# A two-block transformer kernel on one core: modulation weights spread between the layer mixers' products, the last norm and loads in one block, up weights laid out by chunk

## What is computed

```python
for l in range(2):                                   # first block
    mod = silu(c) @ ada_w[l] + ada_b[l]              # 6 x 1024 columns: "modulation"
    h = rms_norm(x) * (1 + mod.scale1) + mod.shift1
    p = h @ w_in                                     # latents, q/k, v, gate, branch gates
    y_mla, y_mlstm = latent attention(p), mLSTM(p)   # 8 heads each
    m = sigmoid(p.br0) * (y_mla @ w_br0) + sigmoid(p.br1) * (y_mlstm @ w_br1)
    x = x + mod.gate1 * (m @ w_out)
    h = rms_norm(x) * (1 + mod.scale2) + mod.shift2
    a, b = split(conv(h @ ffn_w_up))                 # 2 x 2816 columns
    x = x + mod.gate2 * ((gelu(a) * b) @ ffn_w_down)
x = rms_norm(x) * final                              # end of the first block
x = second_block(x, ctx, ...)                        # two recurrences, attention, experts
```

## Time and profile before

| | us |
|---|---|
| median of 3 runs | 2472.73 |
| profiled execution | 2476.21 |
| its span | 2474.4 |
| PE busy | 2041.8 (83%) |
| DVE busy | 1448.3 (59%) |
| ACT busy | 1109.7 (45%) |
| one `ada` piece, issue to landing (median) | 5.2 |
| `final`, issue to landing | 3.5 |
| the second block's `consts`, issue to landing | 4.7 |

### The profile page before, as it was taken

How to read it: one execution, slowest core, us unless ns; L and a number is a source line. 1 busy time by engine, 2 the same in 40 slices (tenths; PEclk the granted TensorE clock), 3 DMA queues, 4 the chain that set the end, 5 groups by cost and what they waited for, 6 DMA issues and landing times. The chain is left out here.

```text
span 2474.4 us, 37498 instructions
## 1 busy us (share of the span) xinstructions
PE 2041.8 (83%) x15206; PEld 1719.4 (69%) x15206; DVE 1448.3 (59%) x1787; ACT 1109.7 (45%) x1308; POOL 144.2 (6%) x134
## 2 busy tenths in 40 slices
PE   4788888698878888789748986798629999999997
PEld 4676666697767666589637774686527878788785
DVE  0274424585446342478425857854438878788786
ACT  0262423464254332356326434212317767677674
POOL 0000000000000000000000632630000000000000
PEclk8798789798989788889878998798759999999998
DMA  8742354453364245264423220000238989899896
GB/s 328 280 149 86 130 194 180 148 193 110 114 228 135 80 162 221 77 232 143 162 86 121 69 74 9 13 18 10 72 137 322 374 291 372 300 348 377 288 371 230
DMA packets 196926, 447.59 MB, mean 181 GB/s; under 512 B 10657, under 2 KB 58401, under 8 KB 196769
## 3 DMA queue, kind: packets, MB, share of 16 engines
q1 hardware_dynamic: 196768, 445.42, 50.7%
HBM read 444.33 MB, written 1.05 MB: 180 GB/s over the span
## 5 line engine op out<-in xcount | busy, mean ns | idle before, releaser
L212 DVE TENSOR_TENSOR me_wlow<-me_w,me_whigh 128x2048 fp32r<-128x2048 f32 x195 | 442.6, 2289 | 101.6 <-ACT me_whigh L207 101.2
L207 ACT ACTIVATE me_whigh<-me_w 128x2048 fp32r<-128x2048 f32 x195 | 372.1, 1918 | 124.3 <-PE ps L220 124.0
L212 DVE TENSOR_TENSOR mix_wlow<-mix_w,mix_whigh 128x1024 fp32r<-128x1024 f32 (+2 forms) x116 | 140.0, 1212 | 154.7 <-ACT mix_whigh L207 154.5
L218 PE MATMUL ps<-me_whigh,me_xhigh 128*128 128x512 f32 x512 | 207.0, 404 | 13.3 <-PEq L119 13.3
L218 PE MATMUL ps<-up_xhigh,up_whigh 128*128 128x256 f32 x704 | 202.9, 288 | 16.8 <-DVE up_wlow L212 16.8
L220 PE MATMUL ps<-me_whigh,me_xlow 128*128 128x512 f32 x512 | 202.2, 395 | 0.0
L219 PE MATMUL ps<-me_wlow,me_xhigh 128*128 128x512 f32 x512 | 202.1, 395 | 0.0
L219 PE MATMUL ps<-up_xlow,up_whigh 128*128 128x256 f32 x704 | 201.6, 286 | 0.0
L220 PE MATMUL ps<-up_xhigh,up_wlow 128*128 128x256 f32 x704 | 201.5, 286 | 0.0
L207 ACT ACTIVATE mix_whigh<-mix_w 128x1024 fp32r<-128x1024 f32 (+2 forms) x116 | 121.2, 1047 | 133.4 <-DMA mix_w<-w_mix 109.0
L218 PEld LDWEIGHTS ps<-up_xhigh,up_whigh 128*128 128x128 f32 x704 | 137.4, 195 | 18.6 <-issue 16.2
(11 more groups left out here) (664 smaller groups left out, 4426.3 us busy)
## 6 DMA issues: line engine op xcount, KB each, us to landing
me_w<-w_exp_gate SPq DMA_DIRECT2D x34, 2048.0 KB, 9.5
me_w<-w_exp_up SPq DMA_DIRECT2D x34, 2048.0 KB, 10.1
me_w<-w_exp_down SPq DMA_DIRECT2D x32, 2048.0 KB, 10.1
mix_w<-w_mix SPq DMA_DIRECT2D x108, 512.0 KB, 4.3
mix_w<-ada_w SPq DMA_DIRECT2D x96, 512.0 KB, 5.2
up_w<-ffn_w_up SPq DMA_DIRECT2D x40, 1024.0 KB, 7.1
ada_w<-ada_first SPq DMA_DIRECT2D x12, 2048.0 KB, 22.3
sec_w<-w_in SPq DMA_DIRECT2D x31, 512.0 KB, 3.7
```

The lines of the kernel that those rows point to most:

```text
L207: return nc.scalar.activation(high, x, ACT.Copy)
L212: return nc.vector.tensor_tensor(low, x, high.bitcast(F32), ALU.subtract)
L218: nc.tensor.matmul(out, lh, rh, start=start, stop=False)
```

## The change

- `Pieces` gets a second ring, `mix_aside`, of three slots for the pieces that are not split; `mix_w` shrinks from five slots to four. SP still issues all fetches from one queue, now in an order sorted by planned times (`fetch_order`).
- The `ada` pieces are spread: four stand at the start, then mostly one after each weight piece (pattern 1, 1, 1, 1, 0, 1, 1, 2, 0). The sum of a chunk is planned later, at +4.4 instead of +3.0 behind the last piece of the chunk, and the bias at +5.2 instead of +4.0.
- Products rotate over three banks, and modulation chunks have bank 3 alone. The last eight products (`out`) use all four.
- `yT[1]` shares the space of `latT`.
- The up weights are laid out on the host so that one chunk is one DMA with a contiguous run in each partition.
- The final norm, its load and the loads of the second block stand in one block, `first_output`.

```diff
+        if wholes:
+            self.aside = core.sb(mem, f"{what}_aside", [P, wholes, KD * P])
...
+    def fetch_order(self):
+        planned, order = self.split_at(), []
+        for split, slots in ((True, self.raws), (False, self.wholes)):
+            users = [p for p, row in enumerate(self.rows) if row[4] == split]
+            for i, p in enumerate(users):
+                before = users[i - slots] if i >= slots else None
+                if before is None:
+                    when = 1.5 * i + 1.0 * split
+                else:
+                    when = planned[before] + 2.0 if split else self.at[before] + 0.8
+                order.append((when, p, before))
+        return sorted(order)
...
-        pieces = Pieces(core, sem, mem, "mix", SLICE, 5, 4, 8.0)
+        pieces = Pieces(core, sem, mem, "mix", SLICE, 4, 4, 8.0, 3)
...
-                pieces.add("ada", spare[0], ada[spare.pop(0)], 0.9, False)
-        for _ in range(12):
-            modulation_piece()
+                pieces.add("ada", spare[0], ada[spare.pop(0)], cost, False)
...
+        pieces.clock = 3.5
+        for _ in range(4):
+            modulation_piece(0.9)
         pieces.clock = max(pieces.clock, 11.0)
...
+            weights(name, i, cost)
+            for _ in range((1, 1, 1, 1, 0, 1, 1, 2, 0)[n % 9]):
+                modulation_piece()
...
-        units = Units(core, sem, "mix", 4, names)
+        units = Units(core, sem, "mix", 3, names)
+        out_units = Units(core, sem, "out", 4, out_names[3 - rest:3] + out_names[:3 - rest] + out_names[3:])
+        ada_units = Units(core, sem, "ada", 1, [f"ada{j}" for j in range(ADA_PIECES // 4)], 3)
...
-                            for s in range(2):
-                                c0 = s * D_FF + j * pairs * P
-                                sp.dma_start(raw[:, j % STAGES, a:b, s * pairs * P:(s + 1) * pairs * P],
-                                             w[:, a:b, c0:c0 + pairs * P])\
-                                    .then_inc(first[n] if j == 0 else landed[j % STAGES], 16)
+                            sp.dma_start(raw[:, j % STAGES, a:b, :], w[j, :, a:b, :])\
+                                .then_inc(first[n] if j == 0 else landed[j % STAGES], 16)
...
+def first_output(core, I, x, coming):
+        with nc.Block(no_gpsimd_drain=True) as block:
+            @block.sync
+            def _(sp):
+                sp.dma_start(final[:, :], I["final"].to_broadcast([P, DM])).then_inc(final_here, 16)
+                for dst, src in coming:
+                    sp.dma_start(dst, src).then_inc(here, 16)
+                sp.wait_ge(here, 16 * len(coming))
```

More of the change, by code:

```diff
@@ L734, in halves, with slot, has_landed @@
         return [self.view(b, slot, p) for b in self.split]
-    def whole(self, p):
-        return self.view(self.raw, p % self.raws, p)
+    def slot(self, p):
+        split = self.rows[p][4]
+        if not split:
+            ring, landed, n, i = self.aside, self.aside_landed, self.wholes, p - self.splits[p]
+        else:
+            ring, landed, n, i = self.raw, self.landed, self.raws, self.splits[p] - 1
+        return ring, landed[i % n], i % n, i // n
+    def whole(self, p):
+        ring, _, slot, _ = self.slot(p)
+        return self.view(ring, slot, p)
+    def has_landed(self, eng, p):
+        _, landed, _, turn = self.slot(p)
+        eng.wait_ge(landed, 16 * (turn + 1))
     def arrived(self, pe, p):
@@ L742, in arrived @@
         else:
-            pe.wait_ge(self.landed[p % self.raws], 16 * (p // self.raws + 1))
-    def fetch(self, sp, between=None):
[L746 to L750, removed]
+            self.has_landed(pe, p)
+    def fetch_order(self):
[6 more added lines that the diff above has]
+                    when = 1.5 * i + 1.0 * split
+                else:
+                    when = planned[before] + 2.0 if split else self.at[before] + 0.8
+                order.append((when, p, before))
+        return sorted(order)
+    def fetch(self, sp, between=None):
+        for n, (_, p, before) in enumerate(self.fetch_order()):
+            if between and n in between:
+                between[n]()
+            split = self.rows[p][4]
+            if before is not None and split:
                 sp.wait_ge(self.low, self.splits[before])
-            elif before >= 0:
+            elif before is not None:
                 sp.wait_ge(self.done, before + 1)
-            sp.dma_start(self.whole(p), src).then_inc(self.landed[p % self.raws], 16)
+            sp.dma_start(self.whole(p), self.rows[p][2]).then_inc(self.slot(p)[1], 16)
     def split_at(self):
@@ L760, in split_at @@
             if row[4]:
-                when, before = self.at[p] - self.lead, p - self.raws
-                if before >= 0:
-                    when = max(when, out[before] + 1.7 if self.rows[before][4] else self.at[before] + 2.5)
+                when = self.at[p] - self.lead
+                if len(users) >= self.raws:
+                    when = max(when, out[users[-self.raws]] + 1.7)
                 if len(users) >= self.parts:
@@ L1043, in opened @@
             if name == "ada":
-                return [f"ada{i // 4}"] if i % 4 == 0 else []
+                return []
             if name == "br":
@@ L1049, in opened @@
             if name == "out":
-                return [f"out{i // 4}{t}" for t in both] if i % 4 == 0 else []
+                return []
             return [f"{name}{t}" for t in both] if i == 0 else []
         names = [unit for name, i, *_ in pieces.rows for unit in opened(name, i)]
-        units = Units(core, sem, "mix", 4, names)
+        units = Units(core, sem, "mix", 3, names)
+        out_names = [f"out{c}{t}" for c in range(2) for t in range(TT)]
+        before_out = names[-3:]
+        rest = len(names) % 3
+        out_units = Units(core, sem, "out", 4, out_names[3 - rest:3] + out_names[:3 - rest] + out_names[3:])
+        ada_units = Units(core, sem, "ada", 1, [f"ada{j}" for j in range(ADA_PIECES // 4)], 3)
         done = pieces.done
@@ L1112, in products @@
                     for t in range(TT):
-                        mm = tokens(f"out{c}{t}", mT, w, 2, 2 * kq, 512, t, kq == 0, kq == 3)
+                        if kq == 0 and c + t < 2:
+                            units.read(pe, before_out[2 * c + t])
+                        elif kq == 0:
+                            ada_units.read(pe, f"ada{ADA_PIECES // 4 - 1}")
+                        mm = tokens(f"out{c}{t}", mT, w, 2, 2 * kq, 512, t, kq == 0, kq == 3, out_units)
                 mm.then_inc(done, 1)
@@ L4009, in second_block @@
         tile_d = nc.dram_tensor("tile_slots", [TILES + 1, P, TT], F32).ap()
-        load(core, "second", [(fvt[:, :], I["second_vectors"])])
         with ExitStack() as mix:
@@ L4218, in layouts @@
     d["first_vectors"], d["next_vectors"] = vectors[0], np.stack(vectors[1:])
+    both = [w.reshape(DM, 2, FF_TILES // 2, 2 * P).transpose(0, 2, 1, 3).reshape(DM, -1) for w in d["ffn_w_up"]]
+    d["ffn_w_up"] = np.stack([w.reshape(KD, P, -1, 4 * P).transpose(2, 1, 0, 3).reshape(-1, P, KD * 4 * P) for w in both])
     d["ada_first"] = modulation_pieces(a["ada_w"][0])
```

112 lines of the change are left out of this document (57 added, 55 removed).

## The result

| | before | after |
|---|---|---|
| median, us | 2474.01 (2467.97 to 2480.93, 4 runs) | 2387.84 (2384.69 to 2395.69, 4 runs) |
| profiled execution; its span | 2476.21; 2474.4 | 2388.65; 2386.5 |
| mean granted clock | 0.889 | 0.907 |

The ratio is 0.9658, with a 95% interval of 0.9628 to 0.9688: the changed kernel is 3.4% faster. The forecast was 2383, with a range of 2345 to 2432.

The account below looks back on a forecast made before the run. PE (83% busy) bounds the kernel, losing time to waits and half clock. Two mixers of -3 + 9 - 8 - 35 give -74, FFN -2, seam -15: -91 from 2476.2 to 2385, 2383 as a median; range 2345 to 2432.

Parts of the forecast that it names:

- The late stage: Mixer's `br`, `branch` and `out` pieces: 94 us work, 9 waits, 3.4 clock, sum 106, so -35 (-39 to -21).
- One sign: Sign of being right: the late stage would start some 2 us sooner in the mixer.
- The early stage: Latents and q/k: sixteen `ada` pieces +7.8, sums +2.9, banks +1.5 and +1.3, some 4 idle covered; +9 (+4 to +14).
- The chunks' bank: Early: next chunk waits for DVE, 0.65 us twice, +1.3; also in the rival that new banks become the wait, chance 0.10.
- The product bank: Early stage: with three banks the second `uq` piece's first tile waits for the last convolution's bank, +1.5 us.
- three more sums: Early stage: three added chunk sums at 0.95 us each, +2.9.
- The middle stage: Attention, mLSTM and thirteen product pieces: 81 us work, 15 idle, 10 clock, sum 106, so -8 (-18 to +3).
- of the 20.5 lost to the clock I give back half: Middle stage: a product or `ada` piece in each gap recovers half the clock loss, leaving 10 us.
- the rival of a clock that stays low: Many small PE gaps keep the clock low: late -21, middle 0, total 2429 us; chance 0.13.
- The start: Mixer's start: four `ada` pieces ahead, four transposes and the sum, first product near 114.5: -3 us (-5 to +1).
- FFN and seam: FFN: up chunk's last part lands sooner, -1 us a layer (0 to -3); seam: earlier norm and loads, -15 (-13 to -16).
- SP starving PE: Rival: `ada` fetches block SP's single queue, PE waits at each of 44 pieces a mixer; 2517 us at w = 1.5; chance 0.04.

Follow-up runs that it names:

- e3_groups_four_slots: Changed kernel with modulation pieces in groups of four, sum and bias at their old planned times, three weight and four modulation slots: 2361.75 us, ratio 0.9559.
- e7_early_sum: Changed kernel with the planned times of a chunk's sum and bias as before the change (+3.0 and +4.0): 2367.37 us, ratio 0.9579.
- e9_shared_banks: Kernel before with rings of three and four slots, four pieces at the start and eleven groups; four banks shared by products and chunks: 2368.86 us, ratio 0.9613.
- e8_seam_and_up: Kernel before with only `first_output` and the up weights by chunk, mixers untouched: 2452.18 us, ratio 0.9922.
- e4_one_ring: Changed kernel, list still spread, with the old single ring of five slots filled in list order: 2471.66 us, ratio 0.9999.
- e1_rings: Kernel before with four weight slots, three modulation slots, sorted fetches and `yT[1]` in `latT`'s space; groups stay: 2475.89 us, ratio 1.0013.
- e5_rings_3_4: Kernel before with three weight slots and four modulation slots; its list, shared banks, up weights and seam stay: 2417.20 us, ratio 0.9783.

## Why the prediction was right, and where it was not

**The sum.** It came out 3 us from the measured span, partly by luck. Over both mixers the start gave 8.5 us more than forecast and the late stage 2.7 more, the middle gave 13.7 less and the early stage cost 4 more; parts that nothing changes gave the 3.2 named above.

**The late stage.** Right in mechanism and sum (-36 against -35, PE without a wait of L957, clock 0.99, no late weight). The terms were off and cancelled: I had 94 us of work, 9 of waits and 3.4 of clock; the window shows 4.1 idle, 1 of clock and 100 of work. Two causes give 4.1 of the 6 us of work; the rest is open. The stage holds 17 pieces and not 14 (I had miscounted the list), and a piece that stands alone between products costs more than the 0.49 that I took from a group of four. In the changed kernel:

```profile
335.52 0.39 PE L220 MATMUL ps<-mix_whigh,mix_xlow 128*128 128x512 f32 x1
335.83 0.64 PE L944 MATMUL ps<-mix_aside,ada_c 128*32 128x128 f32 x16
336.41 0.50 PE L218 MATMUL ps<-mix_whigh,mix_xhigh 128*128 128x512 f32 x1
```

From product to product is 0.89 us, where two matmuls in a row are 0.22 apart: 0.67 for the piece. So measured, a piece costs 0.67 alone and 0.56 in a pair (both late stages), and 0.50 in a four (the late stages of before and of e3_groups_four_slots). One sign failed: the late stage does not start 2 us sooner in the mixer but 7.1 later in the first (208.9 against 201.8 us behind its first piece) and 1.7 sooner in the second, for the reasons that follow.

**The early stage.** +11 against +9. Sixteen pieces (fourteen alone and one pair; matmuls of L1243 part the other pair) are 14 x 0.67 + 2 x 0.56 = 10.5 and not 7.8. The chunks' bank cost 3.6 in e7_early_sum's measure (76.7 to 73.1) and not 1.3, nearly all of it in one wait of 2.90: I priced DVE at 0.37 behind a sum, a row of the late stage, where DVE has little to do, and applied it where the convolution keeps DVE busy. The product bank cost 0.9 of my 1.5. I had priced three more sums; the stage held one before (at 120.65) and holds three now, so it is two, 1.9 us and not 2.9. That makes 16.9. PE idles 6.0 us in the stage, the 4.5 of the two banks among them, against 8.3 before; so some 6.8 us lie in time that was idle before, where I had counted 4. The 1 us that is left goes with the clock, 0.98 against 1.00.

**The middle stage.** The step that failed: "of the 20.5 lost to the clock I give back half". Idle time was as forecast (16.0 against 15). The pieces were miscounted here too: the stage holds 11 and not 14, one fewer than before, which made it lighter by some 1.5 us than I had it. But 23.3 us went to the clock in the first mixer ((1 - 0.80) x 116.57) and 15.5 in the second, so nothing came back in one and 5 in the other. Here the rival of a clock that stays low was right; for the late stage it was wrong, at 0.99. Nor does it take long waits: the falls to 0.50 at 263.8, 277.4 and 301.3 came with waits of 0.71 and 0.72 us. The Trainium skill (TensorE: Matmul & The Clock Gate, "A second HAM failure mode: psum-queue depth-cycling") says that cycling through PSUM banks can leave PE idle briefly so often that its clock goes up and down. Cycling alone does not part the two stages: the products rotate over three banks in both (the eight `out` at the end over four), at 0.80 in the middle and 0.99 late, and over four in e9_shared_banks, at 0.92 and 1.00.

**The start.** -6.6 and -7.9 against -3. The fourth piece began 8.5 us behind the first (102.45), where I had it landed 7.8 behind and multiplied by 8.9. The 32 norm matmuls behind it then took 5.39 us in one go, where I had counted them near four times 2.08, half clock; the clock was at 0.50 up to 106.8 and at 1.00 from there on. The sum ran at 0.95 for the same reason. The term mis-sized is the clock of this stretch.

**FFN and seam.** -0.9 and -2.1, and -14.2: within 1.1 and 0.8 us of the forecast. e8_seam_and_up shows them alone.

**The reason given.** I held the spreading for the cure. e3_groups_four_slots shows that it is only one of two: the illness was a fetch that could not be issued before a multiplication beside it, and either spreading or a fourth slot cures it. Spreading in one ring of five does not (e4_one_ring); whether the separate ring is needed, or only the two slots more, stays open. Of my rivals, SP starving PE was not seen in the changed kernel; in e4_one_ring ACT waits for weights to land and all of the gain is gone. The chunks' bank was a wait in the early stage, as said, and of 2.0 us in four late.

## What to carry to other kernels

Size a ring by the longest run of users that the order puts side by side: three slots for groups of four cost 99 us here (59 with the list of before, from e1_rings to e5_rings_3_4), and one slot moved from a neighbour gave them back. In one queue in list order, pieces that wait on different engines (one on ACT's split, one on PE) hold each other up (e4_one_ring); the cure that was tried is a ring for each and two more slots. And when a buffer has a single copy, put another piece of work between its reader and its next writer in the consumer's own order; the planned time of that reader was worth 20 us, part of it by a clock that wasn't explained.

## What the runs showed of the hardware that I had not expected

A short matmul group between products costs more than its own length: 0.67 us for one piece, 1.11 for two and 1.98 for four, which is 0.44 for each piece and 0.23 once for the group, with the same eight instructions a piece. And equal idle time does not mean equal clock: in the middle stage of the changed kernel PE idles 16.0 us in both mixers, in the same order of the same matmuls, and is granted 0.80 in one and 0.86 in the other, with 5.7 us between their busy times. In e7_early_sum it idles 15.4 us and is granted 0.87.
